# Two-layer transformer and recurrence kernel: the first four weight slabs take x before its norm, and the state-space set-up moves to later slabs

## The reference, cut to what matters

```python
h = rmsnorm(x, norm_mix_pre[l])            # x * rsqrt(mean(x*x by token) + eps) * gain by channel
proj = h @ w_in[l]
q, k, v, u, g_attn, g_ssm = jnp.split(proj, SPLITS, axis=-1)
y_attn = sliding_window_attention(q, k, v, sinks[l], rel_bias) @ w_attn_branch[l]
z = jax.nn.gelu(s5_ssm(u, lam_re[l], lam_im[l], log_dt[l], b_re[l], b_im[l], c_re[l], c_im[l], d_skip[l]))
```

## Time and profile before

| | |
|---|---|
| runs shown | 1448.35, 1448.38, 1450.12 us |
| median | 1448.38 us |
| the profiled execution, its own time | 1448.42 us |
| its span | 1446.6 us |
| matmuls (PE) | 1412.3 us, 98% of the span |
| weight loads (PEld) | 1139.1 us, 79% |
| VectorE (DVE) | 886.2 us, 61% |
| ScalarE (ACT) | 612.4 us, 42% |

### The profile page before, as it was taken

The page is one execution under the profiler, slowest core; times in us unless marked ns, Lnnn a source line. Parts: engine busy times, 40 slices in busy tenths (PEclk is TensorE's granted clock), DMA queues, the critical chain, the costliest instruction groups (busy, mean ns, idle before and its releaser), DMA issues.

```text
span 1446.6 us, 17505 instructions
## 1 busy us (share of the span) xinstructions
PE 1412.3 (98%) x7116; PEld 1139.1 (79%) x7116; DVE 886.2 (61%) x1305; ACT 612.4 (42%) x977; POOL 1.9 (0%) x7
## 2 busy tenths in 40 slices
PE   6999999999999999999999999999999999999997
PEld 5777777787788888887787777778878888888886
DVE  7887764756635354354668888489864443453446
ACT  5453553433312222133336777788642321331232
POOL 0000000000000000000000000000000000000000
PEclk9999999999999999999999999999999999999999
DMA  4222124231323323233132111323233333333223
GB/s 167 88 86 91 59 59 146 73 105 61 116 88 94 109 89 102 87 91 106 51 106 70 52 52 59 102 73 102 88 102 96 94 102 93 97 102 103 87 88 102
DMA packets 37583, 131.60 MB, mean 91 GB/s; under 512 B 4432, under 2 KB 6608, under 8 KB 37248
## 3 DMA queue, kind: packets, MB, share of 16 engines
q1 hardware_dynamic: 37152, 127.16, 28.8%
q0 software_dynamic: 352, 3.34, 0.6%
HBM read 128.39 MB, written 2.10 MB: 90 GB/s over the span
## 4 chain that ended last, share of the span: by engine, by line
PE 85%; DVE 8%; ACT 5%; issue 2%; DMA 0%; SPq 0%; DVEq 0%; ACTq 0%
PE gp L1566 23%; PE gp L1568 23%; PE gp L1567 23%; PE mp L1762 2%; PE mp L1740 2%; PE mp L1773 2%; DVE w_lo L905 2%; ACT w_hi L477 2%; PE mp L1643 1%; PE mp L1645 1%; PE mp L1644 1%; PE mp L1714 1%; PE mp L1685 1%; PE mp L1720 1%; PE gp L1643 0%
## 5 line engine op out<-in xcount | busy, mean ns | idle before, releaser
L1566 PE MATMUL gp<-h_hi,w_hi 128*128 128x512 f32 x944 | 370.6, 393 | 3.8 <-DVE h_lo L949 1.9
L1568 PE MATMUL gp<-h_hi,w_lo 128*128 128x512 f32 x944 | 368.1, 390 | 0.0
L1567 PE MATMUL gp<-h_lo,w_hi 128*128 128x512 f32 x944 | 368.0, 390 | 0.0
L905 DVE TENSOR_TENSOR w_lo<-raw,w_hi 128x1024 fp32r<-128x1024 f32 x202 | 246.5, 1222 | 136.2 <-ACT w_hi L477 135.8
L1566 PE MATMUL gp<-a_hi,w_hi 128*128 128x512 f32 x684 | 268.7, 393 | 1.7 <-DVE w_lo L905 1.6
L477 ACT ACTIVATE w_hi<-raw 128x1024 fp32r<-128x1024 f32 x202 | 211.4, 1050 | 136.2 <-PE gp L1568 77.4
L1567 PE MATMUL gp<-a_lo,w_hi 128*128 128x512 f32 x684 | 266.3, 389 | 0.0
L1568 PE MATMUL gp<-a_hi,w_lo 128*128 128x512 f32 x684 | 266.3, 389 | 0.0
L1566 PEld LDWEIGHTS gp<-h_hi,w_hi 128*128 128x128 f32 x944 | 177.4, 188 | 44.9 <-issue 4.3
L1568 PEld LDWEIGHTS gp<-h_hi,w_lo 128*128 128x128 f32 x944 | 177.5, 188 | 37.3
L1567 PEld LDWEIGHTS gp<-h_lo,w_hi 128*128 128x128 f32 x944 | 177.6, 188 | 36.1
(11 more groups left out here) (279 smaller groups left out, 1588.8 us busy)
## 6 DMA issues: line engine op xcount, KB each, us to landing
raw<-slabs SPq DMA_DIRECT2D x202, 512.0 KB, 3.6
arena<-slabs SPq DMA_DIRECT2D x30, 512.0 KB, 3.6
arena<-x_in SPq DMA_DIRECT2D x4, 512.0 KB, 6.5
arena<-x_in POOLq DMA_DIRECT2D x1, 2048.0 KB, 8.1
out_t<-arena SPq DMA_DIRECT2D x8, 256.0 KB, 2.2
arena<-bias POOLq DMA_DIRECT2D x1, 1024.0 KB, 5.2
arena<-s5b SPq DMA_DIRECT2D x1, 512.0 KB, 9.5
arena<-s5c SPq DMA_DIRECT2D x1, 512.0 KB, 10.5
```

The costliest lines, as they stand in the source:

```text
L905: TT(w_lo[:, n % RING, :], raw(n), w_hi[:, n % RING, :].bitcast(F32), ALU.subtract).then_inc(w_lo_ready, 1)
L1566: pe.matmul(dst, hi, x_hi(t), start=t == 0, stop=False)
L1567: pe.matmul(dst, hi, x_lo(t), start=False, stop=False)
L1568: ins = pe.matmul(dst, lo, x_hi(t), start=False, stop=t == tiles - 1)
```

## The change

x is loaded in the order first quarter, slab 0, the other quarters, slab 1. ScalarE makes `h_hi` and VectorE `h_lo` from x times the gain by channel alone, without the norm by token, and TensorE runs slabs 0 to 3 on them with `gemm`. ScalarE squares all 8 chunks, VectorE folds them with three additions of 128x1024, and TensorE sums and spreads the result inside slab 2. VectorE copies the spread factor to `R`, multiplies the outputs of slabs 0 to 3 by it while it takes them from PSUM (`keep_u`, in a transposed order of tokens, which ScalarE's copy had before), and makes the normalised chunks for slabs 4 and on in the same stretch. The state-space pieces stand at other slabs; the small operations L1000 to L1036 stay behind the last `a_lo`, and slab 6 is now the first that is split behind them. The removed lines of the start (`sum_x_squares`, `pair_sum`) and the renumbered semaphore counts are left out below.

```diff
@@ SyncE
-            for q in range(4):
+            load_x(0)
+            load(slabs[ORDER[0]], 0)
+            for q in range(1, 4):
                 load_x(q)
-            load(slabs[ORDER[0]], 0)
             load(slabs[ORDER[1]], 1)
@@ constants
-        SSM_IN, SSM_OUT, SSM_LOCAL, SSM_TABLE = [7, 11, 13, 15], [12, 14, 16], 9, [6, 7, 8, 9]
-        SSM_DECAY = [6, 9, 12, 14]
+        SSM_WIN, SSM_IN, SSM_OUT, SSM_LOCAL = 6, [10, 13, 15, 16], [14, 15, 16], 12
+        SSM_TABLE, SSM_DECAY = {9: (0, 1), 10: (2, 3)}, [9, 11, 14, 15]
@@ ScalarE
+            for c in range(DC):
+                act.wait_ge(s_x[c // 2], 16)
+                nc.scalar.activation(h_hi[:, c, :], X[:, c, :], ACT.Copy, scale=col("g_mix_pre", c)).then_inc(h_hi_ready, 1)
+                if c == 1:
+                    split(0)
+            split(1)
+            for c in range(4):
+                square("n1", c, X[:, c, :])
+            split(2)
+            for c in range(4, DC):
+                square("n1", c, X[:, c, :])
+            split(3)
             root("n1")
+            split(4)
...
                 nc.scalar.activation(a_hi[:, c, :], tmp[c % 2], ACT.Copy).then_inc(a_hi_ready, 1)
-                if c == 4:
-                    split(2)
+                if c == 0:
+                    split(5)
...
+            n = SLAB["k"]
+            for name in ("k", "v", "q", "gate_a"):
                 for m in range(COUNT[name]):
-                    if n >= 2:
-                        split(n + AHEAD)
+                    split(n + AHEAD)
...
                     evacuate(name, m)
+                    if 0 <= n - SSM_WIN < STEP:
+                        keep_win(n - SSM_WIN)
+                    for ct in SSM_TABLE.get(n, ()):
+                        tables(ct)
@@ VectorE
             dve.wait_ge(s_par, 16)
-            invert_root("n1", keep=False)
+            for c in range(DC):
+                dve.wait_ge(s_x[c // 2], 16)
+                h_low(H_AT["x1"] + c, c, X[:, c, :], col("g_mix_pre", c))
+                if c == 1:
+                    split(0)
+            split(1)
+            fold_squares("n1", 0)
+            split(2)
+            fold_squares("n1", 1)
+            fold_squares("n1", 2)
+            split(3)
+            dve.wait_ge(rms_root, NORM["n1"] + 1)
+            dve.reciprocal(by_token, by_token).then_inc(rms_inverted, 1)
+            split(4)
+            dve.wait_ge(rms_spread, NORM["n1"] + 1)
+            V.run(dve.tensor_copy(R[:, :], mp[:, 5, :]))
+
+            def keep_u(m):
+                TT(U[:, m, :].rearrange("p (s b) -> p s b", s=STEP), take("u", m).rearrange("p (b s) -> p s b", s=STEP),
+                   R[:, :].rearrange("p (b s) -> p s b", s=STEP), ALU.mult).then_inc(out_read, 1)
...
             normalised(0)
-            split(1)
+            keep_u(0)
+            keep_u(1)
             for c in range(1, DC):
                 normalised(c)
                 a_low("n1", c - 1, tmp[(c - 1) % 2])
+                if c == 1:
+                    split(5)
+                if c == 3:
+                    keep_u(2)
                 if c == 6:
-                    split(2)
+                    keep_u(3)
             a_low("n1", DC - 1, tmp[(DC - 1) % 2])
@@ VectorE, behind the small operations L1000 to L1036
-            split(3)
...
-                after[2 + k].append(lambda k=k: by_state(k))
-                after[6 + k].append(lambda k=k: c_power(k + 1))
-            after[3].append(all_turns)
-            after[10].append(local_skip)
-            for ct in range(CT):
-                after[10 + 2 * ct].append(lambda ct=ct: scan_states(ct))
-                after[11 + 2 * ct].append(lambda ct=ct: turn_states(ct))
+                after[4 + k].append(lambda k=k: by_state(k))
+                after[8 + k].append(lambda k=k: c_power(k + 1))
+            after[7].append(all_turns)
+            after[13].append(local_skip)
+            for ct, (n_scan, n_turn) in enumerate(((11, 12), (13, 14), (15, 16), (16, 17))):
+                after[n_scan].append(lambda ct=ct: scan_states(ct))
+                after[n_turn].append(lambda ct=ct: turn_states(ct))
...
-            for n in range(2, SLAB["gate_s"]):
+            for n in range(SLAB["k"], SLAB["gate_s"]):
                 split(n + AHEAD)
                 for piece in after[n]:
                     piece()
@@ TensorE
-            sum_x_squares()
-            spread("n1")
-            start_stage("u", "n1", 2)
-            for n in range(2, SLAB["gate_s"]):
+            gemm("u", 0, 8, 1, h, hl, lambda t: pe.wait_ge(h_lo_ready, H_AT["x1"] + t + 1))
+            gemm("u", 1, 8, 1, h, hl)
+            gemm("u", 2, 8, 1, h, hl, then={1: lambda: mean_of_folded("n1"), 5: lambda: spread("n1")})
+            gemm("u", 3, 8, 1, h, hl)
+            start_stage("k", "n1", 2)
+            for n in range(SLAB["q"], SLAB["gate_s"]):
                 gemm("u", n, 8, 1, a, al)
-                if 3 <= n < 3 + STEP:
-                    turn_win(n - 3)
+                if 0 <= n - SSM_WIN < STEP:
+                    turn_win(n - SSM_WIN)
```

More of the change, by code:

```diff
@@ L328, in build @@
                 _o = OUT[_name] + _k
-                if _name in ("ff", "q2") and 2 <= _k < START_BANKS:
+                if _name == "u":
+                    PLACE[_o] = (mp, _k - 2) if _k >= 2 else (gp, _k)
+                elif _name in ("ff", "q2") and 2 <= _k < START_BANKS:
                     PLACE[_o] = mp, _k - 2
@@ L536, in evacuate @@
             def evacuate(name, m):
[L537 to L540, removed]
+                if name == "gate_a":
                     take(name, m, gate1[m], func=ACT.Tanh, scale=0.5)
@@ L587, in z_chunk @@
                 nc.scalar.activation(h_hi[:, 4 + ct, :], U[:, ct, :], ACT.Copy).then_inc(h_hi_ready, 1)
-            n = 0
-            for name in ("u", "k", "v", "q", "gate_a"):
+            sign_c()
+            act.wait_ge(out_read, OUT["k"])
+            n = SLAB["k"]
+            for name in ("k", "v", "q", "gate_a"):
                 for m in range(COUNT[name]):
-                    if n >= 2:
-                        split(n + AHEAD)
+                    split(n + AHEAD)
                     if n == SLAB["gate_a"]:
-                        act.wait_ge(ca_ready, STEP)
+                        act.wait_ge(win_state, STEP)
                     if n >= SLAB["gate_a"] + 4:
@@ L915, in add_square @@
                     return
-                dve.wait_ge(sq_done, 8 * NORM[kind] - PAIRED + c + 1)
+                dve.wait_ge(sq_done, 8 * NORM[kind] + c + 1)
                 if c >= 2:
@@ L919, in add_square, with fold_squares @@
                 TT(ssum, ssum, sq[c % 2], ALU.add).then_inc(sq_added, 1)
-            def fold_squares(kind):
-                for k in range(FOLDS):
-                    dve.wait_ge(sq_done, 8 * NORM[kind] - PAIRED + 2 * k + 4)
+            def fold_squares(kind, *which):
+                for k in which or range(FOLDS):
+                    dve.wait_ge(sq_done, 8 * NORM[kind] + 2 * k + 4)
                     if k:
@@ L987, in normalised @@
                     dve.wait_ge(a_lo_ready, c - 1)
-                STT(out=tmp[c % 2], in0=X[:, c, :], scalar=col("g_mix_pre", c), in1=mp[:, 5, :], op0=ALU.mult,
+                STT(out=tmp[c % 2], in0=X[:, c, :], scalar=col("g_mix_pre", c), in1=R[:, :], op0=ALU.mult,
                     op1=ALU.mult).then_inc(h_norm, 1)
             normalised(0)
-            split(1)
+            keep_u(0)
+            keep_u(1)
             for c in range(1, DC):
@@ L1036, in _, with product @@
             V.run(TS(f_sign[:, 0, :], f_sign[:, 1, :], -1.0, None, ALU.mult))
[L1037 to L1044, removed]
+            def product(dst, x, re, sign, parts=(pr_a, pr_b)):
+                V.up(TT(parts[0], x, re.unsqueeze(1).unsqueeze(3).to_broadcast([P, 2, PAIRS, 32]), ALU.mult))
+                V.run(TT(parts[1], x[:, ::-1], sign.unsqueeze(3).to_broadcast([P, 2, PAIRS, 32]), ALU.mult))
+                return TT(dst, parts[0], parts[1], ALU.add)
             def by_state(k):
@@ L1057, in c_power @@
                     dve.wait_ge(c_signed, 1)
-                product(ca[:, :, k], ca[:, :, k - 1], a_re, a_sign[:, 1:3, :]).then_inc(ca_ready, 1)
+                    dve.wait_ge(win_turned, 2 * STEP - 2)
+                product(ca[:, :, k], ca[:, :, k - 1], a_re, a_sign[:, 1:3, :], (pr_c, pr_d)).then_inc(ca_ready, 1)
                 dve.wait_ge(ca_ready, k)
@@ L1592, in last_square @@
             def last_square(kind):
-                pe.wait_ge(sq_done, 8 * NORM[kind] - PAIRED + DC)
+                pe.wait_ge(sq_done, 8 * NORM[kind] + DC)
                 for b in range(T // P):
@@ L1652, in a_wait @@
                 return lambda t: pe.wait_ge(a_lo_ready, A_AT[name] + t + 1)
[L1654 to L1661, removed]
             def turn_win(k):
```

31 lines of the change are left out of this document (8 added, 23 removed).

## The result

The changed kernel takes 1452.36 us (median of 9 runs, 1451.46 to 1454.86); before took 1448.46 us in the runs beside it (9 runs, 1448.24 to 1450.12). The ratio is 1.0028, with the interval 1.0019 to 1.0036: slower by 3.9 us, a little more than the 0.2% (2.9 us) that the prediction took as the bound of "same". The time lies inside the range, and the sign is that of the forecast of +1.6 us; but "slower" by more than 0.2%, which is what came, had a chance of only 0.30.

A forecast was written before the change was run, and what follows sets the result against it. Matmuls fill 98% of the span, so TensorE bounds the kernel and gains come only where it waits or runs slowly. -9.8 + 3.1 + 5.9 + 1.6 - 1.6 + 2.4 = +1.6 us gave 1450.0 us, range 1444.5 to 1454.5.

The forecast's parts named there:

- Start: First large matmul at about 11.5 us instead of 21.32, as slab 0 is loaded second: -9.8 us.
- Norm inside slab 2: Sum of folded squares (2.1 us) and spread (1.0 us) now take TensorE's time between matmuls: +3.1 us.
- Wait at slab 6: TensorE waits for slab 6's split behind VectorE's small operations, 23.7 us of chain against 17.9: +5.9 us.
- Clock at slab 6: A stretch of half clock follows the wait before slab 6: +1.6 us, bounds 0 and 3.3.
- The wait at turn_win: by_state(2) is now done before its turn_win, so TensorE's 1.6 us wait there goes: -1.6 us.
- Slab 14: Two more table loads on ScalarE and VectorE's work behind them make TensorE wait before slab 14: 1.7 us.
- First unit: inputs(3) behind slab 16 makes the state chain end later, a wait before the attention's first unit: 0.7 us.
- part 5: Moved state-space pieces: -1.6 us at turn_win, then +2.4 us at slab 14 and the first unit, bounds 0 and 5.
- keep_u, taken at 0.69: VectorE's transposed product, 0.69 us a piece, bounds 0.69 and 1.1; rival that it is slow: 1451.7 us, chance 0.14.
- the clock stays: Rival: clock stays at slab 6 and VectorE closes up sooner, 1446 to 1448.4 us, chance 0.22.
- the early start is kept: Rival: without the slab 6 stall, its half clock and part 5's waits, 1440 us, half the stall 1443; chance 0.12.
- The clock rises one stretch later: Rival: a second slow stretch at the new start, +1.6 us, 1451.6 us, chance 0.08.

The follow-up runs named there:

- the repeated run: The changed kernel once more, unaltered, beside before on the same chip: 1452.42 us (8 runs), ratio 1.0027.

## Why the prediction was right or wrong

The forecast put +1.6 us on the profiled execution; it came out at +2.9 of span and +3.0 in its own time (1451.46 against 1448.42). By the prediction's parts:

- **Start, -9.8:** -10.3 measured (21.32 to 11.05). Right. The slow stretch at the new start took 3.1 us in the profiled execution, as assumed, and 6.1 in the repeated run, which costs 1.4 us more (3.0 us at 0.427 a matmul instead of 0.228), inside the bound of 1.6. In the nine traces used here it lasts 3.1 to 6.1 us.
- **Norm inside slab 2, +3.1:** 2.2. The 16 sums delay the next large matmul by 1.71 (24.82 to 26.53), the spread by 0.35 (29.34 to 29.69), and the matmul behind each restarts 0.09 late. The term was mis-sized because I took the full durations of rows 5 and 6; what the stream loses is the distance of the starts, and the four transposes overlap.
- **Wait at slab 6, +5.9:** 5.96, and 0.57 more in the start stage. The mechanism and its place are right. The step "in the start stage the low parts come just in time" failed by that 0.57, since the keep_u between them take 1.05 us; with R in order this wait isn't there. The chain to the end of the split took 24.8 us (from the end of the spread, 29.94, to 54.73) against 23.7, that of TensorE 18.3 without its waits against 17.9. Of the 1.1 us more on VectorE, four keep_u at 1.05 to 1.08 instead of the 0.65 that this part has (part 6 has 0.69) would alone be 1.7. (23.7 - 17.9 is 5.8; the sum has 5.9.)
- **Clock at slab 6, +1.6:** 1.8. Nine matmuls take 3.86 us there (54.79 to 58.65), against 2.05 at 0.228 each. The row it went by is not a fixed one: behind the same 0.82 us of idle time the clock fell in seven traces and not in two.
- **The wait at turn_win, -1.6:** gone, as said.
- **Slab 14, +1.7:** 1.95, with the two more loads as said. **First unit, +0.7:** 0.66, and 0.27 at outputs(2).
- **Clock behind slab 14:** not in the sum. Part 4 took the half clock as following a pause and priced it at slab 6, but part 5 put a wait of 1.7 us at slab 14 without asking the same question there. Nine matmuls take 3.65 us in that stretch (113.02 to 116.67) instead of 2.05: +1.6.

The measured terms give -10.3 + 2.2 + 6.5 + 1.8 - 1.6 + 1.95 + 1.6 + 0.9 = +3.1, against 2.9 of span. The missing clock stretch alone is larger than the sum's error of 1.3; the mis-sized norm offset a part. The median lies 0.9 us above the profiled execution. The varying stretches of the repeated run are of that size, but no trace shows that they are the whole reason.

**keep_u, taken at 0.69:** wrong, and this was the rival at 0.14. It measured 1.05 to 1.08. The upper bound (1.1) was right; the choice between the bounds failed. It went by the row that was nearest, ScalarE's read of PSUM, but the slow operand was the other one, R in SBUF, for which the text itself said that no row can show it. For that operand the upper value was the one to take. The rule of the Trainium skill, "SBUF — State Buffer", Door 1: The DMA port swizzle, that fp32 accesses which leave a 16-byte line each time pay, is borne out by R's row: 1.06 us against 0.68 with R in order. For PSUM the section names matmuls as what non-contiguous access slows, and VectorE's read of PSUM at 16 bytes a step shows no such cost: it is part of the 0.68 us. By waits, keep_u is worth about 1.0 us of the change.

**Of the rivals,** "the clock stays" and "the early start is kept" fell for this kernel; the second came true in the kernel with its stated condition, the small operations gone from in front of slab 6: there 1445.8, not the 1440 to 1443 of that rival, because slab 14's wait and its half clock remained. With the tables moved too it was 1443.8, and 1441.5 with R in order, which that rival didn't count on. "The clock rises one stretch later" is seen in the repeated run, in the trace of one execution of two. So it was not one case of five. In the profiled execution the forecast's mechanism and keep_u came together with a half clock that the sum lacked, and in the repeated one with the late clock; by their prices (1.0, 1.6 and 1.4 us) any of them carries 1450.0 close to or over 1451.3. Giving them as exclusive cases, with 0.44 in the middle, is why "same" stood at 0.56 and "slower" at 0.30.

## What to carry to other kernels

When a start is moved ahead, write out what each other engine does between the new start and the first slab that waits, and ask of every wait that this leaves, not of the longest alone, whether the clock falls behind it. Work that was free behind a late start has to be given a new cover, or the gain returns as a wait further down; here it took four groups of operations in another order, and R kept in another, to hold 7 of the 10 us. Small costs of one sign that don't exclude each other belong into one sum. Where a stretch of half clock comes in one execution and not in the next, compare traces between two fixed points, such as the first large matmul and the first unit's transposes, before a difference of 1 to 2 us is put down to an edit.

## What the runs showed of the hardware that I had not expected

- A 128x512 product on VectorE takes 1.05 to 1.08 us when one operand is read from SBUF in fp32 at 16 bytes a step, and 0.68 when it is read in order, while a read of PSUM at 16 bytes a step costs nothing (0.68 us in that product, 0.69 in a copy; a plain product is 0.69).
- A wait of 1.95 us was followed by half clock in one execution of the changed kernel (0.50 from 113.1 to 116.5) and not in another (1.00 from 115.5 to 119.0, behind the same wait), and the stretch at the start was 3.1 us or 6.1 with the same work. A wait of 0.82 us at a later norm was followed by it in seven traces of nine.
- With unused matmuls in a wait the clock stayed full (1.00 from 50 to 62 us, 24 of them in 5.75 us), in the one trace that has them, and the median fell by 2.4 us. For slab 6 that is against three traces with the same long wait and the half clock; for slab 14 the repeated run has full clock without them too.
- Going back and forth between sine and tanh costs ScalarE 1.28 us each time (three loads between 90.48 and 99.97).
